# Head queries as plain fp32 products from the row buffers, with heads 3 to 7 between units of picks

## What is computed

```python
q = jnp.einsum('bsd,dk->bsk', h, w_query).reshape(B, S, PEER_HEADS, 2, PEER_HALF)
sc = jnp.einsum('bshpc,hpnc->bshpn', q, sub_keys, preferred_element_type=jnp.float32)
s1, i1 = lax.top_k(sc[..., 0, :], PEER_TOPK)
s2, i2 = lax.top_k(sc[..., 1, :], PEER_TOPK)
...
top_s, sel = lax.top_k(cand_s, PEER_TOPK)
idx = jnp.take_along_axis(cand_i, sel, axis=-1)
gates = jax.nn.softmax(top_s, axis=-1).astype(h.dtype)
...
u = expert_u[ec]
a = jax.nn.gelu(jnp.einsum('cd,chkd->chk', xc, u), approximate=False) * wc
return jnp.einsum('chk,chkd->cd', a, expert_v[ec])
```

## Time and profile before

| | us |
|---|---|
| median of 3 runs | 1531.84 (1531.24 to 1533.04) |
| the profiled execution | 1532.06 |
| its span | 1530.2 |
| PE busy | 1372.8 (90%) |
| DVE busy | 983.4 (64%) |
| ACT, POOL busy | 573.7, 575.0 |
| mean granted clock of PE | 0.968 |

### The profile page before, as it was taken

The page is one execution under the profiler, slowest core; times in us unless marked ns, Lnnn a source line. Parts: engine busy times, 40 slices in busy tenths (PEclk is TensorE's granted clock), DMA queues, the critical chain, the costliest instruction groups (busy, mean ns, idle before and its releaser), DMA issues.

```text
span 1530.2 us, 21440 instructions
## 1 busy us (share of the span) xinstructions
PE 1372.8 (90%) x8012; PEld 1049.2 (69%) x8012; DVE 983.4 (64%) x1895; ACT 573.7 (37%) x1030; POOL 575.0 (38%) x389
## 2 busy tenths in 40 slices
PE   9999999998999999999999989787778777877877
PEld 8999999978999998899998964332333323333332
DVE  3887463554678644484553877777777778777755
ACT  4444354424444434655655432222212223122212
POOL 3444447402344444200304346344444434443440
PEclk9999999999999999999999999899998999898989
DMA  6776773303577653145334699999999999999994
GB/s 232 252 270 247 272 260 138 111 28 115 217 245 277 221 190 138 56 166 188 116 111 138 266 382 423 421 421 422 422 421 421 422 422 421 422 421 421 421 421 202
DMA packets 59776, 427.06 MB, mean 279 GB/s; under 512 B 6640, under 2 KB 6960, under 8 KB 8624
## 3 DMA queue, kind: packets, MB, share of 16 engines
q0 software_dynamic: 36864, 268.45, 42.3%
q1 hardware_dynamic: 22176, 156.38, 28.4%
q10 hardware_dynamic: 656, 1.18, 0.2%
HBM read 424.93 MB, written 1.05 MB: 278 GB/s over the span
## 4 chain that ended last, share of the span: by engine, by line
PE 48%; DMA 26%; issue 11%; DVE 8%; POOL 4%; ACT 2%; DVEq 0%; POOLq 0%; ACTq 0%; SPq 0%
DMA rows_w<-in_expert_uv,arena 18%; DMA keys<-in_expert_uv,arena 7%; PE ps L464 6%; PE ps L459 6%; PE ps L460 6%; PE ps L971 6%; PE ps L975 5%; POOL wlo L341 4%; PE ps L554 3%; PE ps L556 3%; PE ps L555 3%; DVE arena L1868 1%; DVE arena L1505 1%; DMA ring<-in_w 1%; PE ps L507 1%
## 5 line engine op out<-in xcount | busy, mean ns | idle before, releaser
L341 POOL TENSOR_TENSOR wlo<-ring,whi 128x1024 fp32r<-128x1024 f32 x108 | 268.8, 2491 | 458.9 <-ACT whi L1045 458.8
L459 PE MATMUL ps<-nh,whi 128*128 128x256 f32 x1440 | 363.4, 289 | 8.5 <-ACT nh L1063 3.3
L1045 ACT ACTIVATE whi<-ring 128x1024 fp32r<-128x1024 f32 x236 | 244.8, 1056 | 332.1 <-PE ps L464 147.9
L460 PE MATMUL ps<-nh,wlo 128*128 128x256 f32 x1440 | 354.7, 283 | 0.0
L459 PEld LDWEIGHTS ps<-nh,whi 128*128 128x128 f32 x1440 | 275.5, 191 | 15.4 <-issue 5.9
L341 DVE TENSOR_TENSOR wlo<-ring,whi 128x1024 fp32r<-128x1024 f32 x128 | 169.8, 1344 | 172.8 <-ACT whi L1045 168.0
L460 PEld LDWEIGHTS ps<-nh,wlo 128*128 128x128 f32 x1440 | 275.8, 192 | 0.1
L464 PE MATMUL ps<-nl,whi 128*128 128x256 f32 x1440 | 210.4, 286 | 1.3 <-issue 1.1
L464 PEld LDWEIGHTS ps<-nl,whi 128*128 128x128 f32 x1440 | 188.3, 192 | 7.2 <-issue 1.7
L2043 POOL DMA_INDIRECT arena<-in_expert_uv,arena x96 | 112.1, 1168 | 142.7 <-PE ps L975 122.2
L1868 DVE CUSTOM_DVE_ANT_0 arena<-arena 128x1024 f32<-128x1024 f32 x96 | 117.6, 1225 | 38.1 <-DMA arena<-in_expert_uv,arena 34.3
(11 more groups left out here) (329 smaller groups left out, 2294.8 us busy)
## 6 DMA issues: line engine op xcount, KB each, us to landing
ring<-in_w SPq DMA_DIRECT2D x118, 1024.0 KB, 4.8
arena<-in_wmod SPq DMA_DIRECT2D x24, 1024.0 KB, 5.2
small<-in_small SPq DMA_DIRECT2D x2, 938.5 KB, 7.9
arena<-in_expert_uv,arena POOLq DMA_INDIRECT x96, 27.3
h<-in_x SPq DMA_DIRECT2D x2, 512.0 KB, 5.8
keys<-in_keys SPq DMA_DIRECT2D x1, 1024.0 KB, 7.3
...
```

The source lines that it names most:

```text
L341: return v.tensor_tensor(wlo[:, tile % TILES, :], ring[:, tile // 2 % RAW, at:at + TILE], whi[:, tile % TILES, :].bitcast(F32), ALU.subtract)
L459: mm(to, hi[:, k, :], nh[:, k, :], start=(k == 0), stop=False)
L460: mm(to, lo[:, k, :], nh[:, k, :], start=False, stop=False)
L1045: fn(whi[:, tile % TILES, :], ring[:, slot % RAW, at:at + TILE], ACT.Copy).then_inc(S("high_w"), 1)
```

## The change

Each query product is now a plain fp32 product of the slot as it was loaded and of `sq`, 16 of 256 columns per head. `on_vector`, `highs`, `lows` and `split` end at `S_PQ`: no `whi`, `wlo`, `nh` or `nl` is made for the queries. `low_shifted` is gone, and ACT's second shift of `sq` waits only for the scaled blocks.

SP loads the slots of heads 2 to 7 into row buffers 0 to 5 (the arena), and those of 0 and 1 into `ring` (buffers 6 and 7). Head 0 is made by token block: 16 products of 128 columns for block 0, then for block 1, with block 0's scores in between; two banks are opened with zeros ahead. Heads 1 to 3 follow whole, and heads 4 to 7 are made one by one, each behind a unit's 16 weighings (`tensor_order`). A list, `HOMES`, gives each fetch its buffer: 8 that are free from the start (four in `rows_w`, two in `rows_x` over `nh` and `nl`, `rows_s`, `rows_l`), then, in PE's order, the buffer that a query or a weighing frees. `sq` and `keys` are no buffers any more. ACT copies the queries and scores of heads 3 to 7 between its groups of a unit; its load of `final_g` comes after unit 4. DVE dots the first unit 4 rows at a time.

```diff
+def tensor_order():
+    def weighs(first, upto):
+        return [("weigh", g) for g in range(first, upto)]
+    def queries(first, upto):
+        return [("query", hd) for hd in range(first, upto)]
+    order = queries(0, 4) + weighs(0, TK)
+    for hd in range(4, PH):
+        order += queries(hd, hd + 1) + weighs((hd - 3) * TK, (hd - 2) * TK)
+    return order + weighs((PH - 3) * TK, UNITS * TK)
+def query_home(hd):
+    return 6 + hd if hd < RAW else hd - RAW
+def row_homes():
+    homes = [(buffer, None) for buffer in range(PH, SLOTS)]
+    for step, n in tensor_order():
+        homes.append((query_home(n), ("queried", n + 2)) if step == "query" else (homes[n][0], ("weighed", n + 1)))
+    return homes[:UNITS * TK]
...
+LOOPED = 5
...
+        def buffer(s):
             if s < 6:
                 return rows_a[:, s, :]
-            if s == 6:
-                return sq[:, :, :].rearrange("p c t -> p (c t)")
-            if s < 9:
-                return (rows_s, rows_l)[s - 7][:, :]
-            last = W_END - 1
-            if s in (9, 12):
-                return ring[:, (last - (s == 9)) % RAW, :]
-            if s < 15:
-                n = (last - (s < 12)) % (TILES // 2)
-                return rows_w[:, n + (s in (11, 14)) * (TILES // 2), :]
-            return keys[:, :, :].rearrange("p n k -> p (n k)")
+            if s < 8:
+                return ring[:, (weight_slot(S_PQ) + s - 6) % RAW, :]
+            if s < 12:
+                return rows_w[:, s - 8, :]
+            if s < 14:
+                return rows_x[:, s - 12, :]
+            return (rows_s, rows_l)[s - 14][:, :]
+        def expert_rows(g):
+            return buffer(HOMES[g][0])
...
+            def load_query(hd):
+                sp.dma_start(buffer(query_home(hd)), row(a["w"], weight_slot(S_PQ + hd))
+                             ).then_inc(S(f"query_landed{hd}"), 16)
+            sp.wait_ge(S("attended"), 5)
+            sp.wait_ge(S("low_x"), 7 * C)
+            for hd in range(RAW, 2 * RAW):
+                load_query(hd)
...
+            for hd in range(RAW):
+                load(weight_slot(S_PQ + hd))
+            for hd in range(2 * RAW, PH):
+                load_query(hd)
...
+            def open_sums(bank):
+                mm(ps[:, bank, 0:T], zeros[:, :], ones[:, :].unsqueeze(1).to_broadcast([P, TB, P]), start=True,
+                   stop=False, skip_group_check=True)
...
+            def first_scores(b):
+                pe.wait_ge(S("queries_copied"), b + 1)
+                for p in range(2):
+                    last = mm(ps[:, 6 + b, p * P:(p + 1) * P], qT[:, p, b * P:(b + 1) * P], keys[:, p, :],
+                              start=True, stop=True)
+                last.then_inc(S("key_scores"), 1)
+            def first_query():
+                w = query_weights(0)
+                for b in range(TB):
+                    cols = slice(b * P, (b + 1) * P)
+                    for k in range(C):
+                        if b == 0:
+                            pe.wait_ge(S("shifted"), C + k + 1)
+                        for t in range(2):
+                            last = mm(ps[:, first_banks[b], t * P:(t + 1) * P], w[t][:, k, :], sq[:, k, cols],
+                                      start=False, stop=(k == C - 1), skip_group_check=True)
+                        if b == 1 and k == 1:
+                            first_scores(0)
+                    last.then_inc(S("queried"), 1)
+            def query(hd, between):
+                w = query_weights(hd)
+                r = bank(S_PQ + hd)
+                for t in range(2):
+                    for k in range(C):
+                        last = mm(pair(r)[:, t, :], w[t][:, k, :], sq[:, k, :], start=(k == 0), stop=(k == C - 1))
+                    if t == 0:
+                        between()
+                last.then_inc(S("queried"), 1)
...
-            features(S_PQ, split_at=7)
-            key_scores(0)
-            for n in range(4):
-                turn_around(sq, n)
-            for hd in range(1, PH):
-                features(S_PQ + hd, between=(lambda: key_scores(hd - 1)) if hd >= 2 else None)
...
+            first_query()
+            for step, n in tensor_order():
+                if step == "weigh" and n < LOOPED * TK:
+                    weigh(4, n // TK, n % TK, expert_rows(n), n == 0)
+                    if n % TK == 2 * GROUP - 1:
+                        key_scores(3 + n // TK)
+                if step == "query" and n == 1:
+                    query(1, lambda: first_scores(1))
+                    for part in range(2):
+                        turn_around(sq, part)
+                    pe.wait_ge(S("gate_columns"), 1)
+                    for part in range(2):
+                        turn_around(gtb, part)
+                if step == "query" and n >= 2:
+                    query(n, lambda: key_scores(n - 1) if n <= 3 else None)
...
+            with pe.Fori(LOOPED, PH) as j:
+                weigh_unit(4, j)
+            weigh_unit(6, PH, opens=True)
+            with pe.Fori(PH + 1, 2 * PH) as j:
+                weigh_unit(6, j)
...
+                for c in range(C if k == 0 else 0):
+                    act.wait_ge(S("scaled"), c + 1)
+                    fn(nh[:, c, :], sq[:, c, :], ACT.Identity, bias=mod[:, first + c:first + c + 1]
+                       ).then_inc(S("high_x"), 1)
+                if k == 0:
+                    act.wait_ge(S("low_x"), 6 * C)
...
-                act.wait_ge(S("low_x"), (6 + 2 * k) * C)
...
+            def first_out(b):
+                act.wait_ge(S("queried"), b + 1)
+                fn(qT[:, 0:2, b * P:(b + 1) * P], heads(ps[:, (S_PQ % BANKS, 5)[b], 0:T], 2), ACT.Copy
+                   ).then_inc(S("queries_copied"), 1)
+                act.wait_ge(S("key_scores"), b + 1)
+                fn(scores[:, 0, b, :], ps[:, 6 + b, 0:T], ACT.Copy).then_inc(S(("first_copied", "banks_freed")[b]), 1)
...
+                    if j + 3 < PH and q == 0:
+                        query_out(j + 3)
+                    if j + 3 < PH and q == 1:
+                        scores_out(j + 3)
...
-            low_shifted(7, 3 * C)
...
                 choose(0, part)
-            query_lows(3)
             choose(1, 0)
             choose(1, 1)
             choose(1, 2)
-            query_lows(4)
+            dve.wait_ge(S("turned_copied"), 2)
+            dots(0, 0, GROUP)
+            weigh(0, 0, 0, GROUP)
             choose(1, 3)
-            dve.wait_ge(S("turned_copied"), 4)
-            dots(0, 0, 2)
-            query_lows(5)
-            dots(0, 2, 2)
-            query_lows(6)
+            dots(0, GROUP, GROUP)
+            weigh(0, 1, GROUP, GROUP)
             choose(AHEAD, 0)
             choose(AHEAD, 1)
-            query_lows(7)
-            dots(0, GROUP, 2 * GROUP)
-            weigh(0, 0, 0, GROUP)
-            weigh(0, 1, GROUP, GROUP)
             for j in range(UNITS):
+                if j == PH:
+                    dve.wait_ge(S("turned_copied"), 6)
                 for q, first, size in pick_groups(j):
                     if j == 0 and q < 2:
                         continue
-                    if j > 0 or q > 2:
-                        dots(j, first, size)
+                    dots(j, first, size)
...
-            split(n + 1, S_PQ + Q_POOL)
+            split(n + 1, S_PQ)
...
+                home, freed = HOMES[g]
+                if freed:
+                    pool.wait_ge(S(freed[0]), freed[1])
+                if home == SLOTS - 1 and not freed:
                     pool.wait_ge(S("turned"), 4)
-                if g == 8:
-                    pool.wait_ge(S("turned"), 6)
-                if g in (9, 12):
-                    name, n = low_part(2 * (W_END - 2 + (g == 12)) + 1)
-                    pool.wait_ge(S(name), n)
-                if g in (10, 13):
-                    pool.wait_ge(S("tiles_done"), 2 * (W_END - (g == 10)))
-                if g == 15:
-                    pool.wait_ge(S("key_scores"), PH)
-                if g >= SLOTS:
-                    pool.wait_ge(S("weighed"), g - SLOTS + 1)
-                g_rows = expert_rows(g)
-                nc.gpsimd.indirect_dma_start(g_rows, None, a["expert_uv"],
+                nc.gpsimd.indirect_dma_start(buffer(home), None, a["expert_uv"],
```

159 lines of the change are left out of this document (84 added, 75 removed).

## The result

| times in us | before | after |
|---|---|---|
| median | 1531.54 (1529.97 to 1533.04, 4 runs) | 1515.41 (1513.69 to 1517.87, 4 runs) |
| profiled execution, its span | 1532.06, 1530.2 | 1516.74, 1514.9 |
| mean granted clock of PE | 0.968 | 0.974 |

The changed kernel takes 0.989 of the time before (95% interval 0.9877 to 0.9904), 16 us less. The forecast was 12.2 us less, 1519.6; its low end was 1513.

A forecast was written before the change was run, and what follows sets the result against it. The DMA stream of expert-row fetches was taken as the bound. First pick -5.4, loads -7.5, old holes -1.3 and new holes +2.0 sum to -12.2 us, from 1531.84 to 1519.6; forecast 1513 to 1523 (68%), high end 1527.

The forecast's parts named there:

- The bound and the constant: Whole kernel: fetches of expert rows hold DMA at 421 to 423 GB/s; 12.2 us after the last fetch's dots stay untouched.
- First pick: Before the first fetch: DVE's first pick starts at 840.1 instead of 845.5, -5.4 us, bounds -6.3 and 0.
- the rival by which nothing comes of the change: End of the fetch stream: the last DMA engine of sixteen has its own pace and start; 1531.8 us, chance 2%.
- Loads behind the first fetch: DMA after the first fetch: three query loads of 1.05 MB no longer fall there, -7.5 us (3 x 2.49).
- Old holes: DMA stream, 881 to 899 us: idle time while fetches 9 to 15 awaited query-held buffers goes, -1.3 us, bounds 0 and -2.6.
- New holes: DMA stream at unit ends: fetches may wait for buffers freed by queries or weighings, +2 us, bounds 0 and +8.
- the allowance for late landings: Early stream: the walk found no hole, but shortest landings of 8.2 us from issue against margins of 3 led to +2.
- Short ring: Fetch buffers at unit ends: margins go, holes of 6 to 11 us instead of 2; 1523.6 to 1528.6 us, chance 15%.
- the per-unit figure: PE in each unit: 27.5 + 6.9 + 1.0 = 35.4 us of work, under the DMA's 39.8.
- Dear products, slower: PE's query products: at the lower clock a query takes 13.8 us, kernel slower at 1548.0 us, chance 5%.

## Why the prediction was right, point by point

- *The bound and the constant.* The stream stayed at 421 GB/s, and 12.2 us lie behind the last dot in both (1502.71 to 1514.9). Right.
- *First pick*: it moved from 845.52 to 840.10, with the norm 0.56 later. From the scaling to the first fetch it is 22.55 us before and 16.56 now, -6.0 for the forecast's -5.4. A product of 128 columns takes 0.23 us (20 in 4.53, 834.50 to 839.03) where 0.25 was priced; ACT starts the copy of the scores at 839.68, and 839.6 was walked from a norm 0.56 earlier. The run with the scores late shows that this way lies wholly on the path, and with the loads put back it answers the rival by which nothing comes of the change: both moved the end.
- *Loads behind the first fetch*: -7.5 forecast. Between first fetch and last dot the loads of SP's queue and the output's first store come to 3.67 MB before and 0.52 now. These are the two rows, before and changed:

```profile
q1 hardware_dynamic: 576, 3.67, 1.3%
...
q1 hardware_dynamic: 144, 0.52, 0.2%
```

The difference, 3.15 MB, is 7.5 us at 421.5 GB/s. Right. The run that puts three loads back cost 6.1, since there they filled part of the thin start; in the kernel before they did not.

- *Old holes*: -1.3 forecast, within 0 and -2.6. The first 12 us and the next 88 us from the first fetch on, before and then changed, columns as in the earlier trace rows:

```profile
855.32:867.32 12.00, 10.96 (x90) 10.40 (x88) 11.28 (x35) 3.23 (x5) 8.59 (x8) 1.00 0.80 320
867.32:955.32 88.00, 82.02 (x371) 52.59 (x371) 65.88 (x149) 30.33 (x66) 39.88 (x36) 0.96 0.99 405
...
849.89:861.89 12.00, 11.61 (x70) 10.36 (x68) 4.49 (x21) 4.77 (x9) 9.25 (x10) 1.00 0.82 307
861.89:949.89 88.00, 76.75 (x219) 40.27 (x218) 71.01 (x177) 25.28 (x65) 37.97 (x36) 0.96 1.01 422
```

405 GB/s for 88 us is 3.4 us less than the full rate would need, and 422 is the full rate: -3.4, beyond the bound. This term was mis-sized: it took the share of 881 to 899 and not the GB/s, and looked no further than 899, where the trace has another dip, 340 GB/s from 912 to 916. No run tests what made that dip.

- *New holes*: +2 forecast, 0 measured. The margins (850.8 + 2.49 n less the issue) were 8.2 at fetch 12, 5.8 at 20 and 6.0 at 28, where 6, 4 and 3 were walked. The run with a quarter of the late products settles it for heads 4 to 7, the windows for the fetches ahead of them. The step that failed is the allowance for late landings: from 850 to 912 a fetch took 12.4 us at least from issue to landing, and no hole came of it. The rule of the Trainium skill, DMA: Bandwidth & Descriptors, "Anatomy of one DMA — SWDGE (gpsimd) path", weighed there, would have made the sum 2 us lower and so nearer; no run shows a transfer in the 4.4 us estimated from it, only that the allowance wasn't needed.
- *Left out of the sum*: +1.0. The first 12 us are a little thinner than before, 307 GB/s for 320, 0.4 us, though POOL's first fetch instruction takes 1.11 us for 1.83. The last 17.7 us up to the last dot move 193 GB/s for 208, 0.6 us; the prediction carried this end over as it was.
- *Short ring*: no hole of more than 0.2 us came at the unit ends, but the per-unit figure behind it was up to 3.5 us too low for PE, and the reserve is thinner than was told.
- *Dear products, slower*: did not happen. The doubled products show the mechanism, and the price as a sum (25 forecast, 25.5 measured for its parts).

So 16 and not 12: the old holes (2.1 us more than forecast), the new ones (2.0) and the first pick (0.6), less 1.0 for start and end of the stream. That the median fell on the 1515.4 of "all terms at their low bounds" is chance: the old holes went beyond their bound, the first pick stayed short of its own, and 1.0 us stood in no term.
